# The upward product of a gated feed-forward, blocks 3 to 21, as seven quarter products (Strassen's identity) in place of eight

## The chip, the core and the metric

The kernel runs on one core of one Trainium2 chip. The metric is the device time of one execution in microseconds. TensorE (PE) multiplies, VectorE (DVE), ScalarE (ACT) and GpSimd (POOL) do the elementwise work, SyncE (SP) issues most transfers.

## The reference, cut to what matters

The reference is a long network in float32 over 512 tokens and 1024 features: a first mixing block, a feed-forward, an attention with a long convolution, and last a gated feed-forward with a short convolution. Only this last part is touched:

- `h`: the normalized, scaled and shifted state, 1024 features x 512 tokens
- `u = h @ ffn_w_up_2`, 1024 x 5632; its first 2816 columns go through a convolution of three taps along the tokens and a Gelu, and are then multiplied by the last 2816 ("gate")
- `x + gates * (u' @ ffn_w_down_2)`, and a final normalization

The tolerance asks for nearly full float32. So each product is made of three: every operand is split into a high part (rounded to a short mantissa) and a low part (value minus high part), and high x high, high x low and low x high are added up in PSUM.

## The kernel before

Weights come in units of 128 x 1024 floats (512 KB). SyncE loads each into one of four raw buffers (`raw`); ScalarE copies it into a high slot (`wh`, L1225), VectorE, in 17 cases GpSimd, subtracts to get the low slot (`wl`, L1853, L2561). There are four slots of each, and each engine's program calls `weights(upto)`, which brings its own part of the work up to a given unit, three units ahead of TensorE. TensorE waits for a unit's low part when it comes to it; its first matmul of the next unit tells ScalarE that a slot is free (`w_used`). All orders are written out by hand as one program for each engine; every engine works strictly in its program's order and waits at semaphores.

The last part works on blocks of 128 gated features, numbered m = 0 to 21, in two runs: blocks 0 to 11, then the downward product of these 12; blocks 12 to 21, then the downward product of these 10. A block has two units of weights (columns m and 2816 + m, 8 tiles of 128 x 128 each) and two PSUM banks of 512 tokens. TensorE makes each bank with 8 x 3 matmuls of 512 columns (`mm3`, L483). Blocks 0 and 1 are done as halves of 256 columns, since the second half of the normalized state comes later. Then for each block: ScalarE scales the first bank and adds a bias (L1787), VectorE adds the other taps of the convolution (six instructions, L2518), ScalarE applies Gelu (L1790), VectorE multiplies by the second bank (L2523), ScalarE makes the high part (`FFh`, L1794) and GpSimd the low part (`FFl`, L2756). In the downward product VectorE multiplies each bank by a gate (L2536) and GpSimd adds it to the state (L2764).

The state `HTh`, `HTl` is made just before from four buffers `T(4)` to `T(7)` that are used in turn (L2452, L1755, L2444, L2751).

Of the kernel before, what the change touches and what calls it, by code (L numbers as in the profile page):

```python
# [7 lines left out]
F32R = mybir.dt.float32r  # L8
# [7 lines left out]
RAWS = 4  # L16
EARLY = 2
# [131 lines left out]
for _u in range(NU):  # L149
# [8 lines left out]
POOL_LOW = [u for u in range(NU) if u not in PRE and (  # L158
    u < 2 or AT["w_in_2", 0, 1536][0][0] + SLOTS - 1 <= u < AT["w_out_2", 0, 0][0][0] + SLOTS - 1
    or any(u == AT[x][0][0] for x in (((0, 1, 2), 0, 0), ((1, 1, 2), 0, 0), ("w_ff_in", 0, 0))))]  # L160
# [7 lines left out]
class Waits:  # L168
# [5 lines left out]
    def wait_ge(self, name, n):  # L174
        s, before = self.find(name)
        if n > 0 and self.past.get(s.name, 0) < before + n:
# [24 lines left out]
          "p_score": (("p_sc", 24), ("p_ds", 16)),  # L201
# [10 lines left out]
          "v_score": (("sb_sp", 24), ("df_mx", 32)),  # L212
          "v_split": (("sb_ph", 24), ("df_r", 32)),
# [8 lines left out]
          "a_filt": (("f_sin", 3), ("dec", 4)),  # L222
          "a_narrow": (("ff_relu", 32), ("up_a", 22), ("fin_a", 1)),
          "a_exp": (("sb_e2", 24), ("df_e", 32)),
          "g_side": (("dec0", 1), ("tap_ed", 16), ("pg", 17), ("mx_gu", 2)),
          "g_sum": (("eg_add", 2), ("g_add", 12)),
# [34 lines left out]
def program(nc, a):  # L261
    ctx = ExitStack()
    with ctx:
# [51 lines left out]
        Y = at("Y", 160, [P, 4, D])  # L315
        V1 = at("V1", 160, [P, 4, S])
# [145 lines left out]
        def tensor_program(engine):  # L462
# [34 lines left out]

            def weights(name, r, c, occ=0):

                u, o, n = AT[name, r, c][occ]  # L500
                if u != at_unit[0]:
                    assert u == at_unit[0] + 1
                    at_unit[0] = u
                    fresh[0] = u > 0
                    s, n_low = lows(u)
                    e.wait_ge(s, n_low)
                k = u % SLOTS
                return WH[k][:, o:o + n], WL[k][:, o:o + n]

            def held(name, r, c):  # L510

                u, o, n = AT[name, r, c][0]
                e.wait_ge(*lows(u))
                k = u % SLOTS
                return WH[k][:, o:o + n], WL[k][:, o:o + n]

            def high(name, r, c):

                u, o, n = AT[name, r, c][0]
                e.wait_ge("w_hi", highs(u))  # L520
                return WH[u % SLOTS][:, o:o + n]
# [671 lines left out]
            turns[0] = tuple(x for x in range(8) if x not in early_banks) + early_banks  # L1193
            for first_m, count in ((0, 12), (12, 10)):
                for m in range(first_m, first_m + count):
                    for q in range(2 if m > 1 else 0):
# [14 lines left out]
        def scalar_program(engine):  # L1211
# [4 lines left out]
            def weights(upto):  # L1216

                while done[0] <= min(upto, NU - 1):
                    u = done[0]
                    if u not in PRE:  # L1220
                        i, n = RAW_AT["unit", u, 0], UNITS[u][2]
                        e.wait_ge(f"d_raw{i % RAWS}", 16 * (i // RAWS + 1))
                        if u >= SLOTS:
                            e.wait_ge("w_used", u - SLOTS + 1)
                        act(WH[u % SLOTS][:, :n], RAW[i % RAWS][:, :n], ACT.Copy).then_inc(sem("w_hi"), 1)  # L1225
                    done[0] += 1
# [515 lines left out]
            def shifted_half(hf):  # L1742
# [3 lines left out]
                def close(k):  # L1746
                    e.wait_ge(*Z_HALF(k, hf))
                    act(HTh[:, k, c], T(4 + k % 4)[:, c], ACT.Copy).then_inc(sem("n4_hi"), 1)

                for k in KT:  # L1750
                    if k % 4 > 1:
                        e.wait_ge("p_n4", 4 * hf + k // 2 + 1)
                        if k >= 4:
                            e.wait_ge(*LOW_HALF(k - 4, hf))
                        act(T(4 + k % 4)[:, c], PS[:, BANK["n4", hf, k // 2], HALF(k % 2)], ACT.Identity,  # L1755
# [22 lines left out]


            shifted_half(1)  # L1780
            for first_m, count in ((0, 12), (12, 10)):
                for m in range(first_m, first_m + count):
                    weights(unit("ffn_w_up_2", 0, 2816 + m * P) + SLOTS - 1)
                    e.wait_ge("p_up", 2 * m + 1)
                    e.wait_ge("ug_lo", m - 3)
                    z = T(m % 4)
                    act(z, PS[:, BANK["up", m, 0], :], ACT.Identity, scale=pp("ffn_conv_w_2", 22 + m),  # L1787
                        bias=pp("ffn_conv_b_2", m)).then_inc(sem("up_a"), 1)
                    e.wait_ge("uc_v", 7 * m + 6)
                    act(z, z, ACT.Gelu).then_inc(sem("up_g"), 1)  # L1790
                    e.wait_ge("uc_v", 7 * m + 7)
                    if first_m:
                        e.wait_ge("p_dn", 8)
                    act(FFh[:, m - first_m, :], z, ACT.Copy).then_inc(sem("ug_hi"), 1)  # L1794
                if first_m:
                    tables("sqrt_and_others")
                for n in range(2):
                    weights(unit("ffn_w_down_2", (first_m + count - 1) * P, n * S) + SLOTS - 1)
# [23 lines left out]
        def vector_program(engine):  # L1822
# [20 lines left out]
            def weights(upto):  # L1843

                while low[0] <= min(upto, NU - 1):
# [4 lines left out]
                    if u not in POOL_LOW and u not in PRE:  # L1850
                        n, k = UNITS[u][2], u % SLOTS
                        e.wait_ge("w_hi", highs(u))
                        tt(WL[k][:, :n], RAW[RAW_AT["unit", u, 0] % RAWS][:, :n], f32(WH[k][:, :n]),  # L1853
                           ALU.subtract).then_inc(sem("lo_dve"), 1)
# [581 lines left out]
            def shifted_half(hf):  # L2436
# [3 lines left out]
                def close(k):  # L2440
# [3 lines left out]
                    tt(HTl[:, k, c], T(4 + k % 4)[:, c], f32(HTh[:, k, c]), ALU.subtract).then_inc(sem("n4_lo"), 1)  # L2444

                for k in KT:
                    if k % 4 < 2:
                        e.wait_ge("p_n4", 4 * hf + k // 2 + 1)
                        e.wait_ge("ax", 3)
                        if k >= 4:  # L2450
                            e.wait_ge(*LOW_HALF(k - 4, hf))
                        ts(T(4 + k % 4)[:, c], PS[:, BANK["n4", hf, k // 2], HALF(k % 2)], AFF[:, k:k + 1],  # L2452
# [57 lines left out]

            for first_m, count in ((0, 12), (12, 10)):
                for m in range(first_m, first_m + count):
                    z, ps = T(m % 4), PS[:, BANK["up", m, 0], :]
                    weights(unit("ffn_w_up_2", 0, m * P) + SLOTS - 1)
                    e.wait_ge("up_a", m + 1)
                    for i, (w, do, di) in enumerate(CONV):
                        e.wait_ge("uc_v", 7 * m + i)
                        stt(z[:, do], ps[:, di], pp("ffn_conv_w_2", 22 * w + m), z[:, do], ALU.mult,  # L2518
                            ALU.add).then_inc(sem("uc_v"), 1)
                    weights(unit("ffn_w_up_2", 0, 2816 + m * P) + SLOTS - 1)  # L2520
                    e.wait_ge("up_g", m + 1)
                    e.wait_ge("p_up", 2 * m + 2)
                    tt(z, z, PS[:, BANK["up", m, 1], :], ALU.mult).then_inc(sem("uc_v"), 1)  # L2523
                for n in range(2):
                    weights(unit("ffn_w_down_2", (first_m + count - 1) * P, n * S) + SLOTS - 1)
# [23 lines left out]
        def gpsimd_program(engine):  # L2549
# [4 lines left out]
            def weights(upto):  # L2554

                while low[0] <= min(upto, NU - 1):
                    u = low[0]
                    if u in POOL_LOW:
                        n, k = UNITS[u][2], u % SLOTS
                        e.wait_ge("w_hi", highs(u))  # L2560
                        tt(WL[k][:, :n], RAW[RAW_AT["unit", u, 0] % RAWS][:, :n], f32(WH[k][:, :n]),  # L2561
                           ALU.subtract).then_inc(sem("lo_pool"), 1)
# [513 lines left out]
```

## Time and profile before

| | us |
|---|---|
| median of 3 runs | 1457.54 (1457.53 to 1457.76) |
| span of the profiled execution | 1455.8 |
| TensorE busy | 1442.2 (99%) |
| VectorE busy | 815.9 (56%) |
| ScalarE busy | 613.3 (42%) |
| GpSimd busy | 302.6 (21%) |

The span runs from the first to the last instruction of the one profiled execution; the runs' times are of whole executions, and the profiled one has no time of its own beside its span. Durations are those that the profiler recorded. A matmul's recorded duration holds the pipeline's depth: what a matmul costs in a row of them is the distance from one start to the next. The records of VectorE and ScalarE overlap a little for the same reason when instructions follow at once.

### The profile page before, as it was taken

What the parts mean: (1) busy time and instruction counts of PE and PEld (TensorE: products, weight loads), DVE (VectorE), ACT (ScalarE), POOL (GpSimd) and SP (SyncE); (2) the same over time, 40 slices, a digit from 0 to 9 for tenths busy, and PEclk for the clock granted to TensorE, in tenths of its full rate; (3) what the DMA queues carried; (4) which work ended last, traced back from release to release, by engine and by line L of the source; (5) the groups of instructions that cost most, each with busy time, mean ns of one, the idle gap of its engine ahead of it and who ended that gap; (6) DMA issues with size and microseconds to landing.
All of it is one profiled execution on the core that took longest, in us unless ns stands there. A gap on an engine that the chain in (4) does not pass through costs nothing.

```text
span 1455.8 us, 17758 instructions
## 1 busy us (share of the span) xinstructions
PE 1442.2 (99%) x6996; PEld 1186.3 (81%) x6996; DVE 815.9 (56%) x1233; ACT 613.3 (42%) x980; POOL 302.6 (21%) x278
## 2 busy tenths in 40 slices
PE   9999999999999999999999999999999999999998
PEld 7777778888888888888888878888889888888887
DVE  6455666444566543565457437788757454344534
ACT  6545772232453322344345326655545332223332
POOL 1363220102032200121014412115521111121102
PEclk9999999999999999999999999999999999999999
DMA  8351116545264545357327212135614323223221
GB/s 269 119 173 59 59 44 231 203 159 170 89 230 143 169 145 169 116 203 234 130 95 257 73 58 73 59 122 164 221 54 135 102 90 111 90 91 102 96 87 59
DMA packets 54910, 191.13 MB, mean 131 GB/s; under 512 B 6760, under 2 KB 7689, under 8 KB 54443
## 3 DMA queue, kind: packets, MB, share of 16 engines
q1 hardware_dynamic: 48314, 167.06, 35.1%
q0 software_dynamic: 4880, 17.30, 3.5%
q10 hardware_dynamic: 1632, 5.64, 1.1%
q8 instruction: 55, 0.90, 0.2%
q14 instruction: 29, 0.23, 0.0%
HBM read 177.38 MB, written 12.60 MB: 130 GB/s over the span
## 4 chain that ended last, share of the span: by engine, by line
PE 95%; DVE 3%; ACT 1%; issue 1%; POOL 0%; DVEq 0%; ACTq 0%; POOLq 0%
PE PS L483 92%; PE PS L496 3%; DVE TMP L1901 0%; ACT wh L1225 0%; ACT HTh L1247 0%; DVE HTl L1869 0%; DVE TMP L2359 0%; DVE TMP L2321 0%; DVE wl L1853 0%; DVE TMP L1894 0%; ACT TMP L1323 0%; ACT TMP L1321 0%; DVE HTl L2116 0%; ACT HTh L1446 0%; DVE TMP L2109 0%
## 5 line engine op out<-in xcount | busy, mean ns | idle before, releaser
L1853 DVE TENSOR_TENSOR wl<-raw,wh 128x1024 fp32r<-128x1024 f32 x211 | 274.2, 1303 | 313.6 <-ACT wh L1225 313.3
L483 PE MATMUL PS<-HTh,wh 128*128 128x512 f32 (+1 forms) x1088 | 419.2, 386 | 1.0 <-DVE HTl L1869 0.9
L483 PE MATMUL PS<-HTl,wh 128*128 128x512 f32 (+1 forms) x1088 | 415.8, 383 | 0.0
L483 PE MATMUL PS<-HTh,wl 128*128 128x512 f32 (+1 forms) x1088 | 412.0, 383 | 0.0
L1225 ACT ACTIVATE wh<-raw 128x1024 fp32r<-128x1024 f32 x228 | 239.3, 1054 | 273.0 <-PE PS L483 263.1
L483 PEld LDWEIGHTS PS<-HTh,wh 128*128 128x128 f32 x1088 | 204.7, 188 | 47.3 <-issue 8.6
L483 PEld LDWEIGHTS PS<-HTl,wh 128*128 128x128 f32 x1088 | 204.8, 188 | 38.5 <-DVE HTl L1869 0.7
L483 PEld LDWEIGHTS PS<-HTh,wl 128*128 128x128 f32 x1088 | 202.4, 188 | 41.0 <-DVE wl L1853 0.2
L483 PE MATMUL PS<-wl,FFh 128*128 128x512 f32 (+1 forms) x442 | 169.8, 384 | 0.0
L483 PE MATMUL PS<-wh,FFh 128*128 128x512 f32 (+1 forms) x442 | 169.8, 384 | 0.0
L483 PE MATMUL PS<-wh,FFl 128*128 128x512 f32 (+1 forms) x442 | 169.8, 384 | 0.0
L483 PEld LDWEIGHTS PS<-wl,FFh 128*128 128x128 f32 x442 | 83.0, 188 | 16.6
L483 PEld LDWEIGHTS PS<-wh,FFh 128*128 128x128 f32 x442 | 83.0, 188 | 16.5
L483 PEld LDWEIGHTS PS<-wh,FFl 128*128 128x128 f32 x442 | 83.0, 188 | 16.4
L2518 DVE SCALAR_TENSOR_TENSOR TMP<-PS,pp,TMP 128x255 f32<-128x255 f32 (+1 forms) x132 | 52.1, 395 | 73.1 <-ACT TMP L1787 68.9
L2686 POOL TENSOR_TENSOR FFl<-TMP,FFh 128x512 fp32r<-128x512 f32 x32 | 43.4, 1357 | 219.8 <-ACT FFh L1462 219.8
L2756 POOL TENSOR_TENSOR FFl<-TMP,FFh 128x512 fp32r<-128x512 f32 x22 | 28.5, 1295 | 200.7 <-ACT FFh L1794 200.7
L2561 POOL TENSOR_TENSOR wl<-raw,wh 128x1024 fp32r<-128x1024 f32 x17 | 43.9, 2585 | 120.0 <-ACT wh L1225 99.0
L1841 DVE SCALAR_TENSOR_TENSOR raw<-raw,silu_c 128x1024 f32<-128x1024 f32 x48 | 63.9, 1331 | 0.0
L1458 ACT ACTIVATE TMP<-PS 128x512 f32<-128x512 f32 x32 | 19.1, 597 | 62.3 <-PE PS L483 62.3
L2764 POOL TENSOR_TENSOR X<-X,TMP 128x512 f32<-128x512 f32 x14 | 19.7, 1441 | 90.2 <-DVE TMP L2536 90.2
L1790 ACT ACTIVATE TMP<-TMP 128x512 f32<-128x512 f32 x22 | 13.9, 633 | 56.2 <-DVE TMP L2518 56.2
(337 smaller groups left out, 2052.7 us busy)
## 6 DMA issues: line engine op xcount, KB each, us to landing
raw<-in_ws SPq DMA_DIRECT2D x268, 512.0 KB, 3.9
taps<-TMP SPq DMA_DIRECT2D x16, 256.0 KB, 2.5
tab<-in_spec POOLq DMA_DIRECT2D x8, 512.0 KB, 5.7
raw<-taps SPq DMA_DIRECT2D x8, 512.0 KB, 3.8
kd<-TMP POOLq DMA_DIRECT2D x16, 256.0 KB, 6.6
wh<-in_wd POOLq DMA_DIRECT2D x8, 512.0 KB, 4.3
wl<-in_wd POOLq DMA_DIRECT2D x8, 512.0 KB, 5.6
kf<-kd SPq DMA_DIRECT2D x8, 512.0 KB, 4.5
```

Of the source, the lines that this page charges most:

```text
L483: return nc.tensor.matmul(out, l, r, start=start, stop=stop, skip_group_check=True)
L496: return nc.tensor.transpose(out, in_, IDENT)
L1225: act(WH[u % SLOTS][:, :n], RAW[i % RAWS][:, :n], ACT.Copy).then_inc(sem("w_hi"), 1)
L1458: act(T(q % 2), PS[:, BANK["ff", hf, m], :], ACT.Relu).then_inc(sem("ff_relu"), 1)
L1790: act(z, z, ACT.Gelu).then_inc(sem("up_g"), 1)
L1841: stt(r, r, 1.0, SC[:, :], ALU.mult, ALU.mult, accum_out=MOD[:, c:c + 1]).then_inc(sem("mod_acc"), 1)
L1853: tt(WL[k][:, :n], RAW[RAW_AT["unit", u, 0] % RAWS][:, :n], f32(WH[k][:, :n]), ALU.subtract).then_inc(sem("lo_dve"), 1)
L2518: stt(z[:, do], ps[:, di], pp("ffn_conv_w_2", 22 * w + m), z[:, do], ALU.mult, ALU.add).then_inc(sem("uc_v"), 1)
L2561: tt(WL[k][:, :n], RAW[RAW_AT["unit", u, 0] % RAWS][:, :n], f32(WH[k][:, :n]), ALU.subtract).then_inc(sem("lo_pool"), 1)
L2686: tt(FFl[:, q % 16, :], T(2 + q % 2), f32(FFh[:, q % 16, :]), ALU.subtract).then_inc(sem("ff_lo"), 1)
L2756: tt(FFl[:, m - first_m, :], T(m % 4), f32(FFh[:, m - first_m, :]), ALU.subtract).then_inc(sem("ug_lo"), 1)
L2764: tt(x, x, T(4 + q % 4), ALU.add).then_inc(sem("dn_xp"), 1)
```

## The change

From block 3 on, the block's product (256 x 1024 weights by 1024 x 512 state) is seen as 2 x 2 quarters: A11, A12 (128 features, first and second half of the 1024 inputs, of the convolved part), A21, A22 (of the gate), and B11 to B22 of the state, halved by inputs and by tokens. Seven products of quarters take the place of eight (Winograd's form):

- sums of weights, on GpSimd, in place in the raw buffers: S1 = A21 + A22, S3 = A11 - A21, S2 = S1 - A11, S4 = A12 - S2
- sums of the state, once, on GpSimd: T1 = B12 - B11, T2 = B22 - T1, T3 = B22 - B12, T4 = B21 - T2
- products: A11 B11, A12 B21, S2 T2, S1 T1, S3 T3, S4 B22, A22 T4, each 4 x 3 matmuls of 256 columns
- sums of products: two PSUM copies of 256 columns on ScalarE (`kept`) and four additions on VectorE (`first_sum`, `second_sum`, `last_sums`); the last two products of a block are accumulated on top of them

The unit of work in the slots becomes a "use": a whole unit for the rest of the kernel, a half slot (128 x 512) for each of the seven weight operands. TensorE's order in a step is A11(m), S4(m-1), A22(m-1), S2, A12, S1, S3(m). S4(m-1) waits for the second sum, A22(m-1) for the last. Values before the split stay in a buffer `z4` of their own. The diff, cut to its core:

```diff
+HALFSLOT = 512
+SEVEN = range(3, 22)
+LEAD = 5
+RUNS = (range(3, 12), range(12, 22))
+def uses():
+    for u in range(NU):
...
+        out.append(("A11", m))
+        if m > run[0]:
+            out += [("S4", m - 1), ("A22", m - 1)]
+        out += [(n, m) for n in ("S2", "A12", "S1", "S3")]
+        if m == run[-1]:
+            out += [("S4", m), ("A22", m)]
+def ahead(j):
+    i = j
+    while i + 1 < NUSE and i + 1 <= j + LEAD and FREE[i + 1] <= j:
+        i += 1
+    return i
...
+    or USES[j][0] == "A22")]
...
+        Z4 = at("z4", 112, [P, 8, S])
```

TensorE:

```diff
+            def product(n, m, out, xs, start):
+                begin(USE[n, m])
+                h, l = slot(USE[n, m])
+                for k in range(4):
+                    c = slice(k * P, (k + 1) * P)
+                    i = mm3(out, (h[:, c], l[:, c]), xs(k), start and k == 0, k == 3)
+                return i
+            def seven_first(m):
+                for q in range(2):
+                    bank(("up", m, q), "uc_v", 7 * m + 6 + q)
+                product("A11", m, up_bank(m, 0, LEFT_HALF), quarter(0, HALF(0)), True).then_inc(sem("p_part"), 1)
+            def seven_rest(m):
+                product("S2", m, up_bank(m, 1, RIGHT_HALF), turned(1), True).then_inc(sem("p_part"), 1)
+                e.wait_ge(*COPIED(m, 0))
+                product("A12", m, up_bank(m, 0, LEFT_HALF), quarter(4, HALF(0)), False)
+                product("S1", m, up_bank(m, 0, RIGHT_HALF), turned(0), True).then_inc(sem("p_part"), 1)
+                e.wait_ge(*ADDED(m, 0))
+                product("S3", m, up_bank(m, 1, LEFT_HALF), turned(2), True).then_inc(sem("p_part"), 1)
+            def seven_last(m):
+                e.wait_ge(*ADDED(m, 1))
+                product("S4", m, up_bank(m, 0, RIGHT_HALF), quarter(4, HALF(1)), False).then_inc(sem("p_up"), 1)
+                e.wait_ge(*ADDED(m, 3))
+                product("A22", m, up_bank(m, 1, LEFT_HALF), turned(3), False).then_inc(sem("p_up"), 1)
```

ScalarE, which also makes the high parts of T1 to T4 (`turned_high`) in blocks 0 and 1, behind the gated high part:

```diff
+                for m in run:
+                    back = m > run[0]
+                    weights(ahead(at_step(m, 0)))
+                    kept(m, 0)
+                    weights(ahead(at_step(m, 1)))
+                    if back:
+                        centre(m - 1)
+                    weights(ahead(at_step(m, 3)))
+                    if back:
+                        gelu(m - 1)
+                    weights(ahead(at_step(m, 4)))
+                    kept(m, 1)
+                    weights(ahead(at_step(m, 5)))
+                    if back:
+                        gated_high(m - 1, first_m)
+                    weights(ahead(at_step(m, 6)))
```

VectorE, which also makes the low parts of T1 to T4 (`turned_low`) in blocks 1 and 2, behind the gate:

```diff
+                for m in run:
+                    back = m > run[0]
+                    if back:
+                        last_sums(m - 1)
+                    weights(ahead(at_step(m, 0)))
+                    weights(ahead(at_step(m, 1)))
+                    if back:
+                        up_conv(m - 1)
+                    weights(ahead(at_step(m, 3)))
+                    first_sum(m)
+                    weights(ahead(at_step(m, 4)))
+                    if back:
+                        up_gate(m - 1)
+                    weights(ahead(at_step(m, 5)))
+                    second_sum(m)
+                m = run[-1]
+                last_sums(m)
```

GpSimd; each sum of weights waits for the low part of the operand whose place it takes:

```diff
+            def weight_s2(m):
+                e.wait_ge(*lows(USE["A11", m]))
+                e.wait_ge(*summed_at("S3", m))
+                tt(source("S2", m), source("S1", m), source("A11", m), ALU.subtract).then_inc(sem("w_sum"), 1)
+            def weight_s4(m):
+                e.wait_ge(*lows(USE["A12", m]))
...
+                if first_m == 0:
+                    shared_sums()
+                    gated_low(0, 0)
+                    weight_s1_s3(run[0])
+                    weight_s2(run[0])
+                for m in run:
+                    weight_s4(m)
+                    if m - 2 >= first_m:
+                        gated_low(m - 2, first_m)
+                    if m + 1 in run:
+                        weight_s1_s3(m + 1)
+                        weight_s2(m + 1)
+                    weights(USE["A22", m])
+                for m in run[-2:]:
+                    gated_low(m, first_m)
                 for q in range(6 if first_m else 8):
+                    if first_m == 0 and q == 4:
+                        weight_s1_s3(RUNS[1][0])
+                        weight_s2(RUNS[1][0])
```

SyncE, before a raw buffer is loaded anew:

```diff
+                    elif y in PAIR_OF:
+                        m, b = PAIR_OF[y]
+                        for op in (("S3", "A22") if b else ("S4",)):
+                            e.wait_ge(*lows(USE[op, m]))
```

With LEAD = 5 and seven uses a step, `ahead(at_step(m, i))` covers, at its five places, the uses up to S1(m); S3(m); A11(m+1) and S4(m); A22(m); S2(m+1); and on ScalarE a sixth place covers A12(m+1), which VectorE takes at the next step's first place.

## Rows read from the trace of the kernel before

**Rows 1.** Page: busy us with share and count; line shares of the chain.

```profile
PE 1442.2 (99%) x6996; PEld 1186.3 (81%) x6996; DVE 815.9 (56%) x1233; ACT 613.3 (42%) x980; POOL 302.6 (21%) x278
...
PE PS L483 92%; PE PS L496 3%; DVE TMP L1901 0%; ACT wh L1225 0%; ACT HTh L1247 0%; DVE HTl L1869 0%; DVE TMP L2359 0%; DVE TMP L2321 0%; DVE wl L1853 0%; DVE TMP L1894 0%; ACT TMP L1323 0%; ACT TMP L1321 0%; DVE HTl L2116 0%; ACT HTh L1446 0%; DVE TMP L2109 0%
```

**Rows 2.** By stage: stretch, length, busy (count) of PE, PEld, DVE, ACT, POOL, clock, DMA.

```profile
1100.00:1112.00 12.00, 12.00 (x102) 12.00 (x101) 6.20 (x12) 7.33 (x12) 2.05 (x2) 1.00 0.24 76
...
1145.00:1210.00 65.00, 65.00 (x289) 53.81 (x288) 33.13 (x55) 23.66 (x30) 7.77 (x6) 1.00 0.30 97
```

**Rows 3.** TensorE in order of time: start us, us, engine, line, operation, out<-in.

```profile
1109.72 0.28 PE L483 MATMUL PS<-HTh,wl 128*128 128x256 f32 x1
...
1111.88 0.28 PE L483 MATMUL PS<-HTh,wl 128*128 128x256 f32 x1
...
1112.70 0.40 PE L483 MATMUL PS<-HTh,wh 128*128 128x512 f32 x1
...
1129.48 0.39 PE L483 MATMUL PS<-HTh,wl 128*128 128x512 f32 x1
...
1286.11 0.39 PE L483 MATMUL PS<-HTh,wh 128*128 128x512 f32 x1
```

**Rows 4.** One block in order of time: VectorE, then ScalarE, then GpSimd.

```profile
1152.35 2.55 DVE L2518 SCALAR_TENSOR_TENSOR TMP<-PS,pp,TMP 128x255 f32<-128x255 f32 x6 [3.48 <-ACT TMP L1787]
1154.82 1.22 DVE L1853 TENSOR_TENSOR wl<-raw,wh 128x1024 fp32r<-128x1024 f32 x1
1155.95 0.68 DVE L2523 TENSOR_TENSOR TMP<-TMP,PS 128x512 f32<-128x512 f32 x1
...
1163.23 2.54 DVE L2518 SCALAR_TENSOR_TENSOR TMP<-PS,pp,TMP 128x255 f32<-128x255 f32 x6 [3.49 <-ACT TMP L1787]
...
1151.56 0.76 ACT L1787 ACTIVATE TMP<-PS,pp 128x512 f32<-128x512 f32 x1
1154.93 0.63 ACT L1790 ACTIVATE TMP<-TMP 128x512 f32<-128x512 f32 x1 [2.61 <-DVE TMP L2518]
1156.66 0.63 ACT L1794 ACTIVATE FFh<-TMP 128x512 fp32r<-128x512 f32 x1 [1.10 <-DVE TMP L2523]
...
1157.37 1.29 POOL L2756 TENSOR_TENSOR FFl<-TMP,FFh 128x512 fp32r<-128x512 f32 x1 [9.58 <-ACT FFh L1794]
```

**Rows 5.** Groups by shape: count, busy us, mean ns, idle before.

```profile
L2494 DVE TENSOR_TENSOR TMP<-PS,bc 128x256 f32<-128x256 f32 x2 | 0.8, 418 | 0.0
...
L1574 ACT ACTIVATE KTh<-PS 128x256 fp32r<-128x256 f32 x4 | 1.5, 381 | 3.4 <-PE PS L483 3.3
```

**Rows 6.** VectorE and GpSimd at the same times, in four places.

```profile
49.19 2.34 DVE L1853 TENSOR_TENSOR wl<-raw,wh 128x1024 fp32r<-128x1024 f32 x2
...
49.34 4.60 POOL L2603 TENSOR_TENSOR TMP<-TMP 128x512 f32<-128x512 f32 x2 [2.22 <-DVE TMP L1914]
...
787.90 1.81 DVE L2228 TENSOR_TENSOR TMP<-TMP,cs 128x512 f32<-128x512 f32 x1
...
787.89 1.28 POOL L2712 TENSOR_TENSOR TMP<-TMP,cs 128x512 f32<-128x512 f32 x1 [1.03 <-DVE TMP L2225]
...
842.63 0.69 DVE L2228 TENSOR_TENSOR TMP<-TMP,cs 128x512 f32<-128x512 f32 x1
...
842.68 1.80 POOL L2712 TENSOR_TENSOR TMP<-TMP,cs 128x512 f32<-128x512 f32 x1 [7.39 <-DVE TMP L2225]
...
1284.27 2.73 DVE L2536 TENSOR_TENSOR TMP<-PS,bc 128x512 f32<-128x512 f32 x4 [0.80 <-PE PS L483]
1287.69 2.24 DVE L1853 TENSOR_TENSOR wl<-raw,wh 128x1024 fp32r<-128x1024 f32 x1 [0.69 <-ACT wh L1225]
...
1285.04 6.04 POOL L2764 TENSOR_TENSOR X<-X,TMP 128x512 f32<-128x512 f32 x4 [26.61 <-DVE TMP L2536]
```

**Rows 7.** Line 2561 on GpSimd: duration ns min/median/max, first and last start.

```profile
L2561 POOL TENSOR_TENSOR wl<-raw,wh x17: 2371/2418/3290, 11.8 to 1039.4; 128x1024 fp32r<-128x1024 f32 x17
```

**Rows 8.** The transfers into the raw buffers, all stages.

```profile
DMA to landing us min/median/max: 3.5/3.9/10.7
```

More of the change, by code:

```diff
@@ L1780, in scalar_program, with centre @@
             shifted_half(1)
-            for first_m, count in ((0, 12), (12, 10)):
[L1782 to L1794, printed above, removed]
+            def centre(m):
+                e.wait_ge("p_up", 2 * m + 1)
+                e.wait_ge("ug_lo", m - 3)
+                act(T(m % 4), PS[:, BANK["up", m, 0], :], ACT.Identity, scale=pp("ffn_conv_w_2", 22 + m),
+                    bias=pp("ffn_conv_b_2", m)).then_inc(sem("up_a"), 1)
@@ new lines, in kept @@
+            def kept(m, i):
+                e.wait_ge(*PART(m, 2 * i))
+                if i == 0:
+                    act(P1C[m % 2][:, :], PS[:, BANK["up", m, 0], LEFT_HALF], ACT.Copy).then_inc(sem("part_cp"), 1)
+                else:
+                    if m > SEVEN[0]:
+                        e.wait_ge(*ADDED(m - 1, 3))
+                    act(P5C[:, :], PS[:, BANK["up", m, 0], RIGHT_HALF], ACT.Copy).then_inc(sem("part_cp"), 1)
+            for first_m, count in ((0, 12), (12, 10)):
+                run = RUNS[first_m > 0]
+                for m in range(first_m, run[0]):
+                    weights(UP_AHEAD(m, 2816))
+                    centre(m)
+                    gelu(m)
+                    gated_high(m, first_m)
+                    if m < 2:
+                        for i in (2 * m, 2 * m + 1):
+                            turned_high(i)
+                for m in run:
[15 more added lines that the diff above has]
+                m = run[-1]
+                weights(ahead(USE["S4", m]))
+                centre(m)
+                weights(ahead(USE["A22", m]))
+                gelu(m)
+                gated_high(m, first_m)
@@ L1843, in weights @@
             def weights(upto):
[L1845 removed]
+                while low[0] <= min(upto, NUSE - 1):
                     u = low[0]
@@ new lines, in vector_program @@
+            for first_m, count in ((0, 12), (12, 10)):
+                run = RUNS[first_m > 0]
+                for m in range(first_m, run[0]):
+                    weights(UP_AHEAD(m, 0))
+                    up_conv(m)
+                    weights(UP_AHEAD(m, 2816))
+                    up_gate(m)
+                    if m in (1, 2):
+                        for i in (2 * m - 2, 2 * m - 1):
+                            turned_low(i)
+                for m in run:
[13 more added lines that the diff above has]
+                    second_sum(m)
+                m = run[-1]
+                last_sums(m)
+                weights(ahead(USE["S4", m]))
+                up_conv(m)
+                weights(ahead(USE["A22", m]))
+                up_gate(m)
@@ new lines, in weight_s1_s3 @@
+            def weight_s1_s3(m):
+                s1, s3 = source("S1", m), source("S3", m)
+                e.wait_ge(*raw_ready(PAIR[m][1]))
+                if m > SEVEN[0]:
+                    e.wait_ge(*lows(USE["S1", m - 1]))
+                    e.wait_ge(*summed_at("S2", m - 1))
+                else:
+                    e.wait_ge("p_n4", 8)
+                tt(s1, s3, source("A22", m), ALU.add).then_inc(sem("w_sum"), 1)
+                e.wait_ge(*raw_ready(PAIR[m][0]))
+                e.wait_ge(*summed_at("S1", m))
+                tt(s3, source("A11", m), s3, ALU.subtract).then_inc(sem("w_sum"), 1)
```

280 lines of the change are left out of this document (218 added, 62 removed).

## The prediction

> **What bounds the kernel now.** I read the page's busy shares and its chain first: TensorE is busy for 99% of the span, its matmuls are 92% of the chain that ended last, and the clock is at its upper level (2.4 GHz, granted 1.00 in the table by stage) [rows 1, 2]. The product that changes runs from block 3 (block 2 starts at 1112.0, before the first row at 1112.70, and lasts 10.9) at 1122.9 us to 1220.8 (9 blocks), and from 1286.1 for 10 blocks [rows 3]. Next the time order of one block: VectorE, ScalarE and GpSimd all wait for TensorE; between two blocks 10.88 us pass (1163.23 - 1152.35), and GpSimd works 1.29 us of them [rows 4]. So a microsecond taken from TensorE is one gained, as long as the others keep up. They are lightly loaded here (DVE 33 us, ACT 24, POOL 8 of 65) [rows 2], and the change loads just these.
>
> **What TensorE gains.** A block is now 2 x 8 x 3 = 48 matmuls of 512 columns. 74 of them start in 1112.70 to 1129.48, so one takes 226.7 ns, a block 10.88 us. Afterwards it is 7 x 4 x 3 = 84 of 256 columns. The trace has these in the first two blocks: 18 start in 1109.72 to 1111.88, 120 ns each, each with its own weight load, at clock 1.00 [rows 2, 3]. 84 x 0.120 = 10.08 us; one product of 12 is 1.44. Gain 0.80 us a block, 15.2 over 19, if nothing else waits. Blocks 0 to 2 and the downward product stay.
>
> **What the others get.** A step is A11(m), S4(m-1), A22(m-1), S2, A12, S1, S3(m). Per step:
> - ScalarE: 7 high parts of 512 columns at 0.63 us (the FFh rows of that shape), bias, Gelu and high part as now (0.76 + 0.63 + 0.63), two PSUM copies of 256 at 0.38: 7.2 us [rows 4, 5].
> - VectorE: 6 low parts (A22's is on GpSimd), 0.69 alone and 0.60 when the next follows at once (a 1024-wide pair costs 2.34); conv 2.47, gate 0.62, four sums of 256 from PSUM at 0.42 or less: 8.3 us [rows 4 to 6].
> - GpSimd: sums for S4, S1, S3, S2, one gated low part and A22's low part: 6 x 1.26 (1.29 recorded; I take 0.03 of it as overlap when the next follows, as VectorE's records overlap by 0.08) = 7.6 us, from 1.3 now [rows 4].
> Each sum is under 10.08. What decides is that VectorE and GpSimd can't do these at once.
>
> **The shared read path.** Two instructions of exactly these kinds (128x512, both inputs in SBUF) start within 0.05 us of each other in several places. Where GpSimd is first it takes 1.28 and VectorE's takes 1.81 instead of 0.69: held up 1.12. Where VectorE is first, GpSimd's takes 1.80 instead of 1.29: held up 0.51 [rows 6]. VectorE instructions with one input in PSUM are not held: four take 2.73 while GpSimd works, as in any other place [rows 6]. So conv, gate and the four sums are free of it; the 6 low parts and all 6 GpSimd instructions are not. Who gets the path: a waiting VectorE instruction gets it at the end of the GpSimd one in progress (2.24 for a 1024-wide low part, and GpSimd's four take 6.04), and two VectorE low parts in a row (49.19, 2.34 for both) both pass before GpSimd's pair, which takes 4.60 instead of twice 1.29 [rows 6].
>
> The Trainium skill (SBUF — State Buffer, Who interferes with whom) has the path as an exclusive lock, kept for a whole instruction by whichever starts first, the other blocked entirely. The two rows at 787.9 and 842.6 agree; the pair at 49.19 does not, as the waiting GpSimd instruction should have come between. By the page the S4 sum below would start one low part sooner and a step would be 0.2 us shorter.
>
> **A steady step, worked out.** Time 0 is when VectorE begins the last two sums of the block before, just after the second sum that frees S4(m-1) on TensorE. All intervals as above, 0.03 to 0.07 for a signal.
> 1. VectorE: last sums 0 to 0.81; low parts of A12, S1, S3 issued 0.81, 1.41, 2.01, path free 2.57.
> 2. GpSimd's S4 sum needs A12's low part (1.50) but gets the path at 2.57; then gated low part 3.83, S1 5.09.
> 3. TensorE does S4(m-1) from 0.1 to 1.7, bias on ScalarE to 2.53, conv on VectorE 2.61 to 5.07. Then low parts of A11(m+1), S4(m): 5.07 to 6.23 on the path, so S1's sum is 6.2 to 7.5, S3's to 8.75, S2's to 10.04. (If GpSimd is first at 5.09, S2 ends at 9.93: no difference.)
> 4. ScalarE makes S2's high part 10.08 to 10.71. GpSimd meanwhile has started A22's low part at 10.01 and holds the path to 11.14, so S2's low part, ready to go at 10.75, is done at 11.83; next on VectorE behind it stands the second sum (11.74), then time 0 of the next step: 12.1.
> TensorE needs S4(m-1) to S3(m), then A11(m+1), 10.08 us, and waits 2.0 for that second sum at S4(m). I take 12.05 us a step against 10.88 before: 1.17 lost where 0.80 was to be won. The same loop with no hold-up: S2's sum ends 7.9, low part 9.2, next step at 9.6, under TensorE's 10.08. With the first hold-ups but without the collision in point 4, 11.4.
>
> **Starts and ends of the two runs.** Run 1: GpSimd's four shared sums (1024 columns, 2.42 each) go from 1101.8 to about 1112.5 with one VectorE low part between (a 1024-wide low part takes it 2.42 [rows 7]); ScalarE and VectorE add four high parts (1.1) and four low parts (1.13 from start to start, from 1154.82 to 1155.95 [rows 4]), and in block 2 ScalarE makes four new half-width high parts (S2, A12, S1, S3 of block 3) ahead of the bias, so that the bias, now near 1119 (three blocks before the one at 1151.56 [rows 4]), comes near 1126. The last two low parts T3 and T4 then stand behind conv and gate of block 2, to 1134, with two weight low parts and the first sum of block 3 behind them: S3(3) starts near 1137 instead of 1128.7, S4(3) near 1139.9, 17.0 us after the run's start. Run 2: GpSimd's four additions after the first downward product last to 4.9 us after block 12's start (1285.04 + 6.04), S4's sum follows, then S1, S3, S2 of block 13: S4(12) at 12.4 us [rows 3, 6]. A run's last step has neither next block's sums nor S2's low part: 9.5 us; the last two products 2.9. The second step of run 2 lacks a gated low part, 10.8.
> Run 1: 17.0 + 7 x 12.05 + 9.5 + 2.9 = 113.8, before 9 x 10.88 = 97.9: +15.9. Run 2: 12.4 + 10.8 + 7 x 12.05 + 9.5 + 2.9 = 120.0, before 108.8: +11.2. Together +27. Nothing of it is hidden, since TensorE stands on the chain of waits throughout. That the values before the split get a buffer of their own (z4) takes waits from VectorE and ScalarE around 1100: 0, since TensorE is busy 12.00 us of 12 there [rows 2]. The raw weights: b(m+2) is issued after A22's low part (11.3) and lands 3.9 later, at 3.2 of the next step; S1's sum wants it at 5.1 or 6.2. Cover 2 us, so 0; with the longest landing of the queue, 10.7, one step would lose 5 [rows 8].
> The profiled execution has a span of 1455.8 against a median of 1457.5 of the runs, which lies 1.7 above. 1457.5 + 27 = 1484.5; I say 1484.
>
> **Rivals.**
> - B, the hold-ups are there but the collision in point 4 falls away, because high part and low part meet otherwise than worked out: step 11.4 instead of 12.05 in 14 steps, 9 less: 1475. For it: it hangs on 0.7 us of order. Against: GpSimd goes straight from S2's sum to A22's low part, whose high part is ready at 6.4.
> - C, faster: TensorE's rate decides. If the path holds neither (the sums are short enough to fit the gaps), the loop is 9.6 and the step 10.08: -15.2, with 3 + 3 for the starts and 1 for each end: about -7, 1450. It decides once the loop's hold-ups are under 0.5 us together; above 1.3 us the step is past 10.88. For it: the plain busy sums (7.2, 8.3, 7.6) all fit. Against: 6 x 1.12 us of GpSimd and 6 x 0.51 of VectorE make 9.8 us of path time in a step of 10.08, before anyone waits for a signal [rows 6].
> - D, the page's rule: GpSimd gets its turn between two low parts, step 11.8: 3 less, 1481.
> - E, worse: raw weights late or more collisions (each of VectorE's 6 low parts can be held 1.1), step 12.8: +10, 1495.
> - F, steps of 10.3 to 10.5, between B and C: 1.65 less in 16 steps is 26, which leaves the starts' loss and the steps' gain even.
>
> **Chances.** A 0.46, B 0.17, D 0.11, E 0.10: slower 0.84 with these. C 0.12: faster. F 0.04, no change. No change is within 0.2% (2.9 us), about what a measurement of this kernel tells apart. Range 1464 to 1496: it takes in A, B, D, E and steps down to about 10.8 (20 us less over 16 steps), and leaves out C.
>
> **What would show it.** Right: 256-column matmuls 120 ns apart at clock 1.00 in the new stage; gaps of TensorE before S4's first matmul, about 2 us each step, released by VectorE's second sum; a step of 12 us between equal instructions; low parts of 512 with a mean well above 0.69 and GpSimd's sums above 1.29; a gap of 6 to 8 us near 1129. Wrong: low parts at 0.69 beside busy GpSimd, TensorE without gaps from 1140 on (C), or gaps that end with a weight's low part or a DMA instead of that sum.

## The result, and the profile after

The changed kernel takes 1483.9 us (median of 4 runs, 1483.4 to 1484.2), the kernel before in the same series 1457.5: ratio 1.0183, 95% interval 1.0168 to 1.0197. Slower by 26.4 us (1.8%); the prediction had 27 and 1484. The profiled spans differ by 25.8 (1481.6 against 1455.8). Some terms were off against one another; they stand below.

Busy shares from the page of the kernel after, then its chain of waits by engine and by line (they answer to [rows 1]):

```profile
PE 1436.3 (97%) x7680; PEld 1211.1 (82%) x7680; DVE 914.7 (62%) x1389; ACT 666.0 (45%) x1117; POOL 457.0 (31%) x377
...
PE 77%; POOL 7%; DVE 7%; issue 4%; ACT 3%; DMA 1%; SPq 0%; POOLq 0%; ACTq 0%; DVEq 0%
```

By stage (stretch, length, busy of PE, PEld, DVE, ACT, POOL, granted clock, DMA share, GB/s), a steady part of the first run of seven products, to be set against the second row of [rows 2]:

```profile
1150.00:1210.00 60.00, 53.38 (x433) 52.24 (x431) 54.40 (x88) 34.16 (x63) 45.84 (x31) 1.00 0.29 94
```

TensorE was busy for 65.00 us of 65 there and is now for 53.4 of 60. VectorE went from 33 of 65 to 54 of 60, though its own sums come to 8.3 us a step: the rest is instructions that are held up, and a held instruction counts as busy. What TensorE waits for in the whole last part (us in total, times, longest):

```profile
PE PS L610 <- DVE p1c L2776: 20.3, 16, 1.9
PE PS L610 <- ACT p1c L1998: 5.7, 1, 5.7
PE PS L610 <- DVE PS L2783: 4.5, 3, 2.2
PE PS L610 <- DVE HTl L2689: 0.7, 1, 0.7
PE PS L610 <- DVE wl L2099: 0.5, 1, 0.5
```

L2776 is `first_sum`, which S3's product waits for; L2783 is `second_sum`, which S4's waits for; L1998 is `kept`, the copy that A12's waits for.

One steady step in order of time, VectorE first and then GpSimd (start, duration, engine, line, what it does, idle before it); L2099 are low parts, L3100, L3087, L3090 and L3095 the weight sums S4, S1, S3 and S2, L3062 the gated low part, L2866 A22's low part:

```profile
1173.31 1.11 DVE L2099 TENSOR_TENSOR wl<-raw,wh 128x512 fp32r<-128x512 f32 x1 [0.91 <-ACT wh L1410]
1174.34 0.42 DVE L2783 TENSOR_TENSOR PS<-PS,p1c 128x256 f32<-128x256 f32 x1
1174.68 0.42 DVE L2789 TENSOR_TENSOR PS<-PS,p1c 128x256 f32<-128x256 f32 x1
...
1175.47 0.68 DVE L2099 TENSOR_TENSOR wl<-raw,wh 128x512 fp32r<-128x512 f32 x1
1176.07 0.69 DVE L2099 TENSOR_TENSOR wl<-s1w,wh 128x512 fp32r<-128x512 f32 x1
1176.67 1.79 DVE L2099 TENSOR_TENSOR wl<-raw,wh 128x512 fp32r<-128x512 f32 x1
1178.38 2.54 DVE L2759 SCALAR_TENSOR_TENSOR TMP<-PS,pp,TMP 128x255 f32<-128x255 f32 x6
1180.84 2.37 DVE L2099 TENSOR_TENSOR wl<-raw,wh 128x512 fp32r<-128x512 f32 x2
...
1186.08 0.42 DVE L2783 TENSOR_TENSOR PS<-PS,p1c 128x256 f32<-128x256 f32 x1
```

```profile
1172.58 1.29 POOL L2866 TENSOR_TENSOR wl<-raw,wh 128x512 fp32r<-128x512 f32 x1
1176.23 1.68 POOL L3100 TENSOR_TENSOR raw<-raw 128x512 f32<-128x512 f32 x1 [2.36 <-DVE wl L2099]
1177.87 1.74 POOL L3062 TENSOR_TENSOR FFl<-TMP,FFh 128x512 fp32r<-128x512 f32 x1
1179.58 1.29 POOL L3087 TENSOR_TENSOR s1w<-raw 128x512 f32<-128x512 f32 x1
1181.01 1.65 POOL L3090 TENSOR_TENSOR raw<-raw,raw 128x512 f32<-128x512 f32 x1
1182.80 1.55 POOL L3095 TENSOR_TENSOR raw<-s1w,raw 128x512 f32<-128x512 f32 x1
```

Three things are to be read here. Between equal instructions 11.74 us pass (1174.34 to 1186.08), where a block took 10.88 [rows 4]. Low parts of 0.68 take 1.79, 1.11 and, two of them, 2.37, wherever a GpSimd instruction lies beside them; conv, with an input in PSUM, takes 2.54 as before, beside GpSimd's busiest stretch. And the S4 sum, which could start at 1176.23, takes 1.68: it gets the path when the low part in progress ends, at about 1176.7, between two low parts that follow each other. All 17 steps between 1140 and 1410 show the same (1.78 or 1.79 for that third low part).

### The profile page after: what moved, and what is told of

The parts are those of the page before. It is cut to its first block, busy times and chain, and to the rows that moved or that the text cites. A ratio compares the mean times of both kernels' runs of the same rounds, so it can differ in the third digit from the quotient of the medians.

```text
span 1481.6 us, 19740 instructions
## 1 busy us (share of the span) xinstructions
PE 1436.3 (97%) x7680; PEld 1211.1 (82%) x7680; DVE 914.7 (62%) x1389; ACT 666.0 (45%) x1117; POOL 457.0 (31%) x377
## 4 chain that ended last, share of the span: by engine, by line
PE 77%; POOL 7%; DVE 7%; issue 4%; ACT 3%; DMA 1%; SPq 0%; POOLq 0%; ACTq 0%; DVEq 0%
PE PS L610 75%; PE PS L623 2%; POOL raw L3090 2%; POOL raw L3095 2%; POOL FFl L3062 2%; DVE wl L2099 1%; POOL s1w L3087 1%; DVE TMP L2759 1%; ACT wh L1410 1%; POOL raw L3100 1%; ACT wh L1415 1%; DMA raw<-in_ws 1%; DVE PS L2783 1%; DVE wl L2096 0%; DVE PS L2791 0%
## 5 line engine op out<-in xcount | busy, mean ns | idle before, releaser
L2096 DVE TENSOR_TENSOR wl<-raw,wh 128x1024 fp32r<-128x1024 f32 x173 | 225.4, 1307 | 268.4 <-ACT wh L1415 268.2
L610 PE MATMUL PS<-HTh,wh 128*128 128x512 f32 (+1 forms) x1012 | 368.3, 365 | 11.9 <-ACT p1c L1998 5.7
L610 PE MATMUL PS<-HTl,wh 128*128 128x512 f32 (+1 forms) x1012 | 363.1, 360 | 0.0
L610 PE MATMUL PS<-HTh,wl 128*128 128x512 f32 (+1 forms) x1012 | 359.2, 360 | 0.0
L2099 DVE TENSOR_TENSOR wl<-raw,wh 128x512 fp32r<-128x512 f32 x95 | 106.1, 1131 | 35.9 <-ACT wh L1410 35.9
L610 PE MATMUL PS<-th,wh 128*128 128x256 f32 x304 | 88.0, 290 | 20.7 <-DVE p1c L2776 20.3
L1410 ACT ACTIVATE wh<-raw 128x512 fp32r<-128x512 f32 x114 | 70.1, 623 | 45.6 <-POOL raw L3095 28.8
L610 PE MATMUL PS<-tl,wh 128*128 128x256 f32 x304 | 86.2, 284 | 0.0
L610 PE MATMUL PS<-th,wl 128*128 128x256 f32 x304 | 86.1, 283 | 0.0
L610 PEld LDWEIGHTS PS<-th,wh 128*128 128x128 f32 x304 | 58.6, 193 | 24.2 <-DVE p1c L2776 23.5
```

Of the source, the lines that this page charges most:

```text
L610: return nc.tensor.matmul(out, l, r, start=start, stop=stop, skip_group_check=True)
L1410: act(slot(j)[0], source(kind, u), ACT.Copy).then_inc(sem("w_hi"), 1)
L2096: tt(l, RAW[RAW_AT["unit", x, 0] % RAWS][:, :UNITS[x][2]], f32(h), ALU.subtract).then_inc(sem("lo_dve"), 1)
L2099: tt(l, source(kind, x), f32(h), ALU.subtract).then_inc(sem("lo_dve"), 1)
```

## The experiments

In the first batch the kernel before took 1457.6 us (7 runs, 1456.0 to 1457.8), in the second 1457.55 (7 runs, 1457.3 to 1458.9).

**Do the reads hold up, or the amount of GpSimd's work?** Each weight sum is replaced by two memsets of the same 512 columns, the second of which waits for the first (the sums are left out, so this kernel multiplies other numbers). One run.

```diff
-                tt(s1, s3, source("A22", m), ALU.add).then_inc(sem("w_sum"), 1)
+                nc.gpsimd.memset(x, 1.0).then_inc(sem("w_first"), 1)
+                e.wait_ge("w_first", firsts[0])
+                nc.gpsimd.memset(x, 1.0).then_inc(sem("w_sum"), 1)
```

> GpSimd's four sums of weights are replaced by two memsets each of the same 512 columns (the sums are left out, so the seven products multiply other numbers); GpSimd keeps about its time and all its signals, but these instructions read nothing from SBUF. Theory (the shared read path sets the step of 11.73 us): VectorE's low parts are no longer held by the sums, nor the sums by them; the loop through both engines is under TensorE's rate, step 10.1 to 10.3, time 1456 to 1462. Rival 1 (GpSimd's amount of time in the loop, whoever shares the path): step stays 11 to 11.7, time 1472 to 1484. Rival 2 (TensorE's own chain of products and sums, GpSimd beside the point): step 11.7, 1484, here and in the next kernel.

Measured: 1455.5 us (span 1453.3). VectorE and GpSimd of that kernel in the same place of a step:

```profile
1180.29 0.68 DVE L2099 TENSOR_TENSOR wl<-s1w,wh 128x512 fp32r<-128x512 f32 x1
1180.89 0.68 DVE L2099 TENSOR_TENSOR wl<-raw,wh 128x512 fp32r<-128x512 f32 x1
...
1180.43 0.53 POOL L3083 MEMSET raw<- 128x512 f32 x1 [2.79 <-DVE wl L2099]
1181.02 0.53 POOL L3086 MEMSET raw<- 128x512 f32 x1
```

GpSimd is busy from 1180.43 to 1181.55, right beside two low parts that take 0.68 each. Two memsets last 1.12 together, a sum 1.29 alone, so the amount is nearly the same; four times the 0.17 that is missing makes 0.7 us a step, less than the 1.66 that the step lost. The step is 10.08 (the second sum at 1168.48 and 1178.56), TensorE's own rate, and its waits for `first_sum` are down from 20.3 us to one of 1.3. The hold-up is a matter of GpSimd's reads, and it is the whole of the loss per step. That the time is still only 2 us under the kernel before (a single run, and the 7 runs of that kernel lie within 1.8 us) says something else: the starts and ends eat most of the 15.2 us. The two runs of blocks took TensorE 98.6 and 105.3 us, against 97.9 and 108.8 before.

**How much is left without the sums?** The same sums cut to 8 columns (so the rest of each is left out, and the numbers are others here too); one run.

```diff
-                tt(s3, source("A11", m), s3, ALU.subtract).then_inc(sem("w_sum"), 1)
+                tt(s3[:, 0:8], source("A11", m)[:, 0:8], s3[:, 0:8], ALU.subtract).then_inc(sem("w_sum"), 1)
```

> The same four sums of weights are cut to 8 columns (but for the first S1), so GpSimd has neither the time nor the reads. Theory: step 10.1, TensorE without gaps but at the starts, 1455 to 1459, close to the kernel with memsets. Rival 1: also about 1457, and then it is the kernel with memsets that tells the two apart. Rival 2: 1484. If TensorE's 256-column matmuls cost more than 120 ns in this mix, the step is above 10.1 without gaps.

Measured: 1451.75 us, 3 below what was expected, step 10.08, waits of 5.0, 1.6, 0.7 and 0.5 us left in the whole part. Not all of the 6 us to the kernel before is the form's: TensorE comes to block 3 at 1121.75, where it was 1122.9, though nothing that these kernels do ahead of it is quicker (over all the kernels of this document the start of block 2 lies between 1110.8 and 1113.0). The two runs of blocks take 98.6 and 103.4 us against 97.9 and 108.8. So this form with these orders is worth 4.7 us, and not 15.2, even where its weight sums cost next to nothing: 10.5 are lost at the starts and ends.

**Is it the place of the gated low part?** It goes behind S2's sum.

```diff
                     weight_s4(m)
-                    if m - 2 >= first_m:
-                        gated_low(m - 2, first_m)
                     if m + 1 in run:
                         weight_s1_s3(m + 1)
                         weight_s2(m + 1)
+                    if m - 2 >= first_m:
+                        gated_low(m - 2, first_m)
```

> GpSimd's gated low part goes behind the S2 sum of the next block instead of ahead of S1's; nothing else. Theory: the loop runs low part of A12, S4, S1, S3, S2 sums, S2's high and low part, second and last sums; the gated low part's 1.3 to 1.7 us leave it, S2's sum ends sooner, its low part then meets the gated low part in progress instead of A22's: step 10.6, time 1464 to 1468. Rival 1 (GpSimd is simply full, order is worth nothing): step 11.7, 1484. Rival 2 (TensorE's chain): 1484.

Measured: 1483.8 us (1483.3 to 1484.2), ratio 1.018 (1.0163 to 1.0197). The expectation was wrong by all it had. GpSimd of this kernel in one step:

```profile
1174.77 1.68 POOL L3100 TENSOR_TENSOR raw<-raw 128x512 f32<-128x512 f32 x1 [0.66 <-DVE wl L2099]
1179.39 1.80 POOL L3087 TENSOR_TENSOR s1w<-raw 128x512 f32<-128x512 f32 x1 [2.94 <-DMA raw<-in_ws]
1181.34 1.55 POOL L3090 TENSOR_TENSOR raw<-raw,raw 128x512 f32<-128x512 f32 x1
```

S1's sum stands 2.94 us for its raw weights (11.4 us in 6 of the steps between 1140 and 1220). A22's low part ended at 1174.1, and the buffer that it frees is filled 5.2 later; in four of the six steps it is 3.8 to 3.9 later. In the kernel of the change S1's sum starts 5.7 after that low part's end (1173.87 to 1179.58), so the cover was 1.9 us, as the prediction had it (2). The move takes more than that: the gated low part (1.74) no longer stands between, and A22's low part, now behind it, ends later by its 1.29 and is itself held (1.73 instead of 1.29).

**Is it the collision of A22's low part with S2's?** A22's low part goes from GpSimd to VectorE.

```diff
-    or any(j == AT[x][0][0] for x in (((0, 1, 2), 0, 0), ((1, 1, 2), 0, 0), ("w_ff_in", 0, 0)))
-    or USES[j][0] == "A22")]
+    or any(j == AT[x][0][0] for x in (((0, 1, 2), 0, 0), ((1, 1, 2), 0, 0), ("w_ff_in", 0, 0))))]
```

> A22's low part is made by VectorE instead of GpSimd; nothing else. Theory: only the collision of that low part with S2's goes (1.11 recorded against 0.69), the low part itself falls into VectorE's idle 0.9 us: step 11.3, time 1476 to 1479. Rival 1 (GpSimd's amount): it has one of six instructions less, 1.5 us: step 10.2 to 10.5, 1460 to 1465. Rival 3 (VectorE's amount of work): 0.6 us more a step, 1492.

Measured: 1481.2 us (1479.8 to 1481.4), ratio 1.016 (1.0144 to 1.0175). VectorE of this kernel:

```profile
1171.86 0.41 DVE L2775 TENSOR_TENSOR p1c<-PS,p1c 128x256 f32<-128x256 f32 x1
1172.19 1.43 DVE L2098 TENSOR_TENSOR wl<-raw,wh 128x512 fp32r<-128x512 f32 x1
1173.54 0.67 DVE L2764 TENSOR_TENSOR TMP<-TMP,PS 128x512 f32<-128x512 f32 x1
1174.14 0.68 DVE L2098 TENSOR_TENSOR wl<-raw,wh 128x512 fp32r<-128x512 f32 x1
1174.74 0.42 DVE L2782 TENSOR_TENSOR PS<-PS,p1c 128x256 f32<-128x256 f32 x1
```

S2's low part (1174.14) takes 0.68 now: the collision of the prediction's point 4 is gone. But A22's low part stands ahead of it on the same engine and is itself held by S2's sum (1.43), so the step is 11.66 (p1c at 1171.86 and 1183.52) and not 11.3. GpSimd stands idle for 3.56 us of this step ahead of S4's sum, so its amount does not bound the step either.

**Both moves, and a wait.** A22's low part on VectorE, and the gated low part behind the sums, but, by a wait that neither kernel above has, not before VectorE has cut the next S2's low part.

```diff
                         weight_s2(m + 1)
+                        if m - 2 >= first_m:
+                            e.wait_ge(*lows(USE["S2", m + 1]))
+                    if m - 2 >= first_m:
+                        gated_low(m - 2, first_m)
```

> Two moves together: the low part of A22 goes to VectorE (as in the kernel that gave 1481.2), and GpSimd's gated low part goes behind its four weight sums of a step and waits until VectorE has cut the low part of the next S2. Theory: the step is the alternation of VectorE's low parts with GpSimd's sums over the shared read path; with the gated low part out of the stretch between S4's sum and S2's, the raw weights are there (they are asked for earlier) and the low parts are held four times and not five. Step about 10.75 (before: 10.88), 18 steps: 1467, with the starts' and the ends' gaps left. Rival 1, the raw weights are late again, as when the gated low part stood behind S2's sum alone: step 11.7, 1481 to 1484. Rival 2, VectorE's amount (one more low part of 0.69 to 1.79 per step) decides: step 12.0, 1487.

Measured: 1470.9 us (1469.3 to 1471.1), ratio 1.0087 (1.007 to 1.0104), 13 us less than the change. Its GpSimd, and the two longest waits of its TensorE:

```profile
1173.27 1.30 POOL L3061 TENSOR_TENSOR FFl<-TMP,FFh 128x512 fp32r<-128x512 f32 x1 [1.83 <-DVE wl L2098]
1175.20 1.68 POOL L3099 TENSOR_TENSOR raw<-raw 128x512 f32<-128x512 f32 x1 [0.62 <-DVE wl L2098]
1177.04 1.54 POOL L3086 TENSOR_TENSOR s1w<-raw 128x512 f32<-128x512 f32 x1 [0.16 <-DMA raw<-in_ws]
```

```profile
PE PS L609 <- DVE p1c L2775: 9.7, 17, 1.9
PE PS L609 <- ACT p1c L1997: 5.9, 1, 5.9
```

The gated low part now lies beside the second and the last two sums of VectorE, which have an input in PSUM and are not held; the raw weights are there to within 0.16 in this step. The step is 10.87 (second sum at 1173.12 and 1183.99). I had 10.75 and 1467: the direction and the order of size were right. The two single moves gained 0.1 and 2.7 us; together, and with the wait, they gain 13. The traces say why the single ones gained so little: the one ran into the raw weights, the other into VectorE's order. The two moves without the wait were not run, so how the 13 us divide is not shown.

**The starts.** The seven products begin with the sixth block instead of the fourth, nothing else.

```diff
-SEVEN = range(3, 22)
-RUNS = (range(3, 12), range(12, 22))
+SEVEN = range(5, 22)
+RUNS = (range(5, 12), range(12, 22))
```

> The seven products begin at the sixth block (index 5) instead of the fourth, so that weights are loaded well ahead and the gated high parts of the first blocks are long done when the run of seven products begins. Nothing else is changed; the first gated low parts are issued ahead of the first weight sums. Theory: two steady steps at 11.73 go back to 10.88 us (-1.7) and the start's gap before the copies (5.70 us at 1132.97 in the kernel of the change) goes, because ScalarE no longer has a backlog there: about 1477. Rival 1, the gap belongs to the start of any run of seven products, wherever it stands (first weight sums, load of the first raw weights): it moves to the sixth block and only the two steps come back, 1482. Rival 2, the two steps were as cheap as before because their cover was full: 1484.

Measured: 1474.4 us (1472.6 to 1475.6), ratio 1.0114 (1.0099 to 1.0129): 9.5 less than the change, 2.6 below the expectation. The profiled spans differ by 7.7 only (1473.9 against 1481.6). The wait for the copy is 1.7 us where it was 5.7, and the clock is 1.00 all the way from 1100 to 1240, which I had not reckoned with (below): with the two steps (1.7), 4.0 of wait and 1.4 of clock make 7.1 of the 8.0 us that TensorE takes less from block 2 to the first downward matmul. The step is unchanged (second sum at 1178.32 and 1190.05: 11.73). So most of the first start's loss belonged to the neighbourhood of the first blocks and not to the form. That it was ScalarE's and VectorE's parts of T1 to T4 fits the rows there (two low parts of 1024 columns in 2.83 us at 1131.39, and the copy behind them at 1132.55) but was not tested by itself.

**All of it.** Both moves, the start at the sixth block, and S4's sum of block 12 ahead of GpSimd's additions.

```diff
                     if first_m == 0 and q == 4:
                         weight_s1_s3(RUNS[1][0])
                         weight_s2(RUNS[1][0])
+                        weight_s4(RUNS[1][0])
```

> The two moves of the kernel with A22's low part on VectorE and the gated low part behind S2's; and the seven products begin at the sixth block; and in the second run the sum S4 of its first block is issued ahead of GpSimd's additions to the downward product. Theory: 1467 less about 5 us of the first start's gap less 1.9 and 1.2 us of the second's: 1458 to 1460, no gain over the kernel before. Rival, the steps stay at 11.7 as in both single moves: 1472 to 1475.

Measured: 1464.3 us (1462.6 to 1466.4), ratio 1.0046 (1.0031 to 1.0061): 20 us less than the change and still 7 more than the kernel before, where I had put 1458 to 1460. One step of its VectorE:

```profile
1175.99 0.42 DVE L2782 TENSOR_TENSOR PS<-PS,p1c 128x256 f32<-128x256 f32 x1
...
1178.52 1.78 DVE L2098 TENSOR_TENSOR wl<-raw,wh 128x512 fp32r<-128x512 f32 x1
...
1184.31 1.43 DVE L2098 TENSOR_TENSOR wl<-raw,wh 128x512 fp32r<-128x512 f32 x1
...
1186.86 0.42 DVE L2782 TENSOR_TENSOR PS<-PS,p1c 128x256 f32<-128x256 f32 x1
```

The step is 10.87, the same as a block of the kernel before, and nothing is won in it; VectorE works without a pause (58.0 us of 60 from 1150 to 1210) with two low parts still held by 1.1 and 0.75. What is left of the starts and ends (waits of 4.8, 1.8 and 0.7 us) is then all loss. I had counted on 10.75, and not on the clock, which falls here too, in the second start after a wait of 2.46 us. S4's sum ahead of the additions gave 0.5 us and not 3.1: the second run of blocks takes 112.4 us, and 112.9 with both moves alone, since one wait of 2.46 and the lower clock stand in the place of waits of 1.94 and 1.10. No version that computes the right product is faster than the kernel before. The one with sums of 8 columns gives an idea of the most that these orders could give: 4.7 us, and by an estimate some 4 more with the later start (3.3 of wait and 2.2 of clock saved, which is 24 matmuls at 0.21 instead of 0.12; twice 0.80 given up). No run shows that sum.

## Why the prediction was right, point by point

- **TensorE's gain: right.** 256-column matmuls stand 0.12 apart at clock 1.00, and with the path free the step is 10.08, as worked out.
- **The path between VectorE and GpSimd: right in kind and size** (1.79 - 0.68 = 1.11 held, against 1.12 of [rows 6]), and shown to be the cause by the memsets. The Trainium skill (SBUF — State Buffer, Who interferes with whom) says that a VectorE instruction with two SBUF inputs contends with GpSimd instructions that read SBUF and not with those that only write it; the memset run agrees (0.68 beside 0.53 + 0.53).
- **Who gets the path next: wrong.** I had two low parts in a row pass ahead of a waiting GpSimd instruction, from the pair at 49.19 [rows 6]; this was rival D, the rule that the prediction took from the Trainium skill, and for S4's sum it was right in all 17 steps. In time from VectorE's last sums (1174.68), predicted and measured ends: S4's sum 3.83 and 3.2, gated low part 5.09 and 4.9, S1's sum 7.5 and 6.2, S3's 8.75 and 8.0, S2's 10.04 and 9.7, second sum's start 11.74 and 11.4. The step is 11.74 and not 12.05; D had 11.8. The row at 49.19 had parts of 1024 columns; why GpSimd did not come between there is open.
- **The collision of A22's low part with S2's: right.** S2's low part takes 1.11 (1173.31) behind the GpSimd instruction of 1172.58 that ends at 1173.87. Taking it away alone gains no more than 2.7 us, since the work moves to the engine that is late.
- **Where TensorE waits: wrong place, and a size too large.** I named the second sum before S4's product and 2.0 us. TensorE waits for the first sum before S3's, 1.3 us a step (1.6 from start to start, where 0.12 is usual, so 1.5 lost); it comes to S4's product at the moment the second sum is done. I had followed the chain to its last link and not asked at which earlier link TensorE meets it first.
- **Run 1: predicted 113.8 us, measured 111.2** (1123.54 to the first downward matmul at 1234.69). S3(3) was to start near 1137 (it started at 1137.4), S4(3) 17.0 after the run's start (16.7), T4's low part to end at 1134 (1134.2). The gap of 6 to 8 us near 1129 is the 5.70 that ends at 1132.97; it stands before A12's product, behind ScalarE's copy, and not before S3's. So the time of S3(3) is partly luck: the first sum that I made it wait for was done at 1135.75, TensorE came later than that, and 1.4 us of its delay are the lower clock, which no term of mine has. The seven steps from S4(3) to S4(10) took 81.5 us and not 84.4, six at 11.74 and the first 11.1; the last, from one second sum (1221.28) to the next (1231.24), took 9.96 and not 9.5, with one whole unit of the downward product cut ahead of the sum.
- **Run 2: predicted 120.0, measured 120.7** (1300.00 to 1420.65). S4(12) came 12.2 after the start (12.4). The seven steps gave 2.2 back here, but the last step took 11.1 (second sums at 1404.62 and 1415.71) and not 9.5, and the last products 4.4 and not 2.9. In the last step VectorE has cut two whole units of the downward product ahead of the second sum, which I had left out; these are its rows:

```profile
1411.71 0.42 DVE L2776 TENSOR_TENSOR p1c<-PS,p1c 128x256 f32<-128x256 f32 x1
1412.84 1.23 DVE L2096 TENSOR_TENSOR wl<-raw,wh 128x1024 fp32r<-128x1024 f32 x1 [0.72 <-ACT wh L1415]
1413.98 0.68 DVE L2765 TENSOR_TENSOR TMP<-TMP,PS 128x512 f32<-128x512 f32 x1
1414.58 1.22 DVE L2096 TENSOR_TENSOR wl<-raw,wh 128x1024 fp32r<-128x1024 f32 x1
1415.71 0.43 DVE L2783 TENSOR_TENSOR PS<-PS,p1c 128x256 f32<-128x256 f32 x1
```

  TensorE waits 2.20 us for that sum, and this is TensorE from the wait to the end of a slow stretch:

```profile
1416.20 0.58 PE L610 MATMUL PS<-HTh,wh 128*128 128x256 f32 x1 [2.20 <-DVE PS L2783]
...
1417.01 0.41 PE L610 MATMUL PS<-HTh,wh 128*128 128x256 f32 x1
1417.22 0.41 PE L610 MATMUL PS<-HTl,wh 128*128 128x256 f32 x1
...
1419.69 0.28 PE L610 MATMUL PS<-tl,wh 128*128 128x256 f32 x1
1419.81 0.28 PE L610 MATMUL PS<-th,wl 128*128 128x256 f32 x1
```

  0.21 us from start to start instead of 0.12: TensorE runs at its lower clock (1.2 GHz) for the 16 matmuls up to 1419.57, 1.5 us lost. I had no such term.
- **Costs put at nothing.** The shared sums cost 0.7 us that I had at 0: the first of them holds a VectorE low part of HTl (3.29 us at 1100.11), and TensorE waits 0.71 for it at 1103.45. The downward products take what they took (65.3 us between the runs before and after). The raw weights cost nothing in the steps, as predicted, and their cover was as thin as the 2 us that I had (1.9, as worked out above).

Sum: 0.65 before run 1, 13.25 in run 1 (111.15 - 97.9), 11.85 in run 2 (120.65 - 108.8), 0.05 behind: 25.8, the whole difference of the spans. Against the 27.1 of the prediction's own sum, the 14 steps are 5.0 less (2.8 and 2.2); the other way went 1.5 of clock in the last products, 1.6 and 0.5 in the two last steps and 0.65 ahead of run 1; the rest is small. That the total came out closer than its terms is luck: steps put 0.31 too high stood against terms that I did not have. The likeliest case, A, named the right causes, and D the right order on the path.

## What to carry to other kernels

Where work is moved onto GpSimd beside a busy VectorE, count path time and not busy time: in this kernel a GpSimd instruction that reads SBUF and a VectorE instruction with two SBUF inputs took turns and held each other, VectorE by up to 1.11 us and GpSimd by up to 0.5, and the held time counts as busy; put them beside instructions that have an input in PSUM. An instruction that looks like a pure obstacle may be the cover of a transfer, so ask of every move what was hidden behind it: here two moves that gained 0.1 and 2.7 us alone gained 13 together with one wait. A saving of 7% per step that needs 19 steps to collect is mostly gone when the starts and ends of its stretches cost 10 of the 15 us even with sums of next to nothing; work these out first.

## What was not expected of the hardware

The clock. After the wait of 5.70 us that ends at 1132.97 the granted clock is 0.50 up to about 1136.2, then 1.00, and it costs some 1.4 us; after the wait of 2.20 that ends at 1416.20 it is 0.50 as well, up to 1419.57. The waits of 1.3 us in each step, and one of 1.94 at 1307.85, were followed by 1.00 throughout. By stage, in the kernel after (columns as above):

```profile
1134.00:1136.00 2.00, 2.00 (x11) 2.00 (x11) 1.75 (x4) 0.00 (x0) 1.11 (x1) 0.50 0.00 0
...
1307.80:1310.00 2.20, 2.15 (x18) 2.15 (x19) 0.00 (x0) 0.00 (x0) 2.06 (x3) 1.00 0.61 162
...
1416.20:1418.00 1.80, 1.80 (x8) 1.80 (x9) 0.74 (x3) 1.06 (x1) 0.73 (x1) 0.50 0.81 271
```

The same wait of 1.94 us, before the same product of block 12, went the other way in the kernel that starts at the sixth block. Its clock behind the wait that ends at 1300.08:

```profile
1300.08:1303.40 3.32, 3.32 (x16) 3.32 (x16) 0.46 (x1) 1.12 (x3) 3.18 (x3) 0.51 0.57 158
```

There it cost nothing, since VectorE and GpSimd set the pace: the second sum of block 12 starts 11.73 us after the start of that run of blocks, and 11.75 in the kernel after, where the clock stayed at 1.00. So the length of a wait does not tell by itself whether the lower clock follows it, and here the lower clock cost time only where the rest waited for TensorE. Where it does, a wait of a few microseconds can cost some 1.5 us more than the view of waits gives it. The spread of a kernel's runs goes with it in one case: the four runs with all moves took 1462.6, 1463.3, 1465.2 and 1466.4 us at mean granted clocks of 0.999, 0.998, 0.996 and 0.994. What tells a wait that is followed by the lower clock from one that isn't was not tested.
